# Spare identity matmuls on TensorE inside the four attention cores of a five-block transformer kernel

## What is computed

```python
logits = einsum('bqhd,bkhd->bhqk', q, k) * scale + bias      # causal, band or top-k mask
p = softmax(logits)                                          # B adds a sink to the sum
o = einsum('bhqk,bkhd->bqhd', p, v)
x = x + o @ w_out
x = x + relu(rms_norm(x) @ w_up) ** 2 @ w_down
```

## Time and profile before

| | |
|---|---|
| median of three runs | 1817.03 us |
| the profiled execution | 1824.34 us |
| its span (first to last instruction) | 1822.5 us |
| PE busy | 1723.5 us, 95% |
| DVE, ACT, POOL busy | 1154.3, 930.6, 218.5 us |
| attention cores, about | 36, 37, 34 and 36 us of the span |

### The profile page before, as it was taken

The page is one execution under the profiler, slowest core; times in us unless marked ns, Lnnn a source line. Parts: engine busy times, 40 slices in busy tenths (PEclk is TensorE's granted clock), DMA queues, the critical chain, the costliest instruction groups (busy, mean ns, idle before and its releaser), DMA issues.

```text
span 1822.5 us, 26545 instructions
## 1 busy us (share of the span) xinstructions
PE 1723.5 (95%) x9368; PEld 1459.2 (80%) x9368; DVE 1154.3 (63%) x1958; ACT 930.6 (51%) x1504; POOL 218.5 (12%) x297
## 2 busy tenths in 40 slices
PE   7999999999999988899998899998799999789998
PEld 6889988887788876698886698887598888569887
DVE  6676454556678757755666666567765654875665
ACT  5462354644444554654446554447754445465443
POOL 3005420100000002300003400003100000320000
PEclk9999999999999988999999999999999997899999
DMA  8440046546456442256664156553266664235662
GB/s 273 130 139 1 1 124 179 182 128 196 146 177 196 161 146 81 82 184 186 189 190 151 55 178 193 186 160 120 67 219 188 188 186 127 81 95 184 190 190 81
DMA packets 158450, 270.29 MB, mean 148 GB/s; under 512 B 15181, under 2 KB 42268, under 8 KB 158364
## 3 DMA queue, kind: packets, MB, share of 16 engines
q1 hardware_dynamic: 156843, 263.35, 46.6%
q0 software_dynamic: 1504, 5.79, 0.9%
q10 hardware_dynamic: 16, 0.00, 0.0%
HBM read 268.04 MB, written 1.07 MB: 148 GB/s over the span
## 4 chain that ended last, share of the span: by engine, by line
PE 82%; DVE 8%; ACT 4%; issue 3%; POOL 2%; DMA 0%; DVEq 0%; SPq 0%; ACTq 0%; POOLq 0%
PE p_AC L2479 11%; PE p_AC L2481 11%; PE p_AC L2480 11%; PE p_UP L2479 6%; PE p_UP L2481 6%; PE p_UP L2480 6%; PE p_TP L2512 5%; PE p_UP L2512 5%; PE p_TP L2546 3%; PE p_UP L2513 2%; PE p_TP L2513 2%; PE p_AC L1152 1%; DVE t_wl L1993 1%; ACT t_lg L1520 1%; PE p_UP L1140 1%
## 5 line engine op out<-in xcount | busy, mean ns | idle before, releaser
L1993 DVE TENSOR_TENSOR t_wl<-t_raw,t_wh 128x1024 fp32r<-128x1024 f32 (+2 forms) x525 | 610.5, 1169 | 484.1 <-ACT t_wh L1412 481.4
L1412 ACT ACTIVATE t_wh<-t_raw 128x1024 fp32r<-128x1024 f32 (+2 forms) x525 | 529.6, 1014 | 602.4 <-PE p_AC L2481 290.7
L2479 PE MATMUL p_AC<-t_wh,t_uTh 128*128 128x512 f32 (+1 forms) x612 | 241.5, 395 | 9.5 <-DVE t_uTl L2172 3.9
L2481 PE MATMUL p_AC<-t_wh,t_uTl 128*128 128x512 f32 (+1 forms) x612 | 239.7, 392 | 0.0
L2480 PE MATMUL p_AC<-t_wl,t_uTh 128*128 128x512 f32 (+1 forms) x612 | 239.7, 392 | 0.0
L2479 PE MATMUL p_UP<-t_wh,t_hT 128*128 128x512 f32 (+3 forms) x576 | 227.4, 395 | 4.0 <-DVE t_hT L2038 4.0
L2481 PE MATMUL p_UP<-t_wh,t_hT 128*128 128x512 f32 (+3 forms) x576 | 224.1, 389 | 0.0
L2480 PE MATMUL p_UP<-t_wl,t_hT 128*128 128x512 f32 (+3 forms) x576 | 223.8, 389 | 0.0
L2512 PE MATMUL p_TP<-t_hT,t_wh 128*128 128x512 f32 x384 | 144.4, 399 | 0.0
L2512 PE MATMUL p_UP<-t_hT,t_wh 128*128 128x512 f32 x384 | 144.0, 398 | 0.0
L2479 PEld LDWEIGHTS p_AC<-t_wh,t_uTh 128*128 128x128 f32 x612 | 115.8, 189 | 34.9 <-DVE t_uTl L2172 8.0
(11 more groups left out here) (346 smaller groups left out, 2820.4 us busy)
## 6 DMA issues: line engine op xcount, KB each, us to landing
t_raw<-in_w_up SPq DMA_DIRECT2D x128, 512.0 KB, 3.9
t_raw<-in_w_down SPq DMA_DIRECT2D x128, 512.0 KB, 3.9
t_raw<-in_w_in SPq DMA_DIRECT2D x72, 512.0 KB, 3.6
t_raw<-in_w_up SPq DMA_DIRECT2D x88, 256.0 KB, 3.9
t_raw<-in_a_w_in SPq DMA_DIRECT2D x26, 512.0 KB, 4.3
t_raw<-in_w_down SPq DMA_DIRECT2D x44, 256.0 KB, 3.2
t_raw<-in_a_w_out SPq DMA_DIRECT2D x16, 512.0 KB, 3.4
t_raw<-in_b_w_in SPq DMA_DIRECT2D x12, 512.0 KB, 3.8
```

What stands on the lines that cost most here:

```text
L1412: A_(wh[:, c % SPL, 0:size(c)], raw[:, c % RAW, 0:size(c)], ACT.Copy).then_inc(high_done, 1)
L1993: V.tensor_tensor(wl[:, c % SPL, 0:n], raw[:, c % RAW, 0:n], wh[:, c % SPL, 0:n].bitcast(F32), ALU.subtract).then_inc(split_done, 1)
L2479: M(outs[t], a_hi, w_hi[:, k, :], start=first and k == 0, stop=False)
L2481: ins = M(outs[t], a_lo, w_hi[:, k, :], start=False, stop=last and k == ch.nk - 1)
```

## The change

`spare(count)` issues matmuls of the 128x128 identity with itself, into the last 128 columns of bank 0 of `TP`, which nothing reads and no transpose uses. A matmul is two records, so `spare(2)` is four.

```diff
@@ -2599,6 +2599,11 @@
             def att_core(n):
                 c = att_list[n]
                 hb, pb = AH * n, PAIRS * n
+
+                def spare(count):
+                    for _ in range(count):
+                        M(tpb(0, P, 3 * P), ident[:, :], ident[:, :], start=True, stop=True)
+
                 for i in range(PAIRS + 3):
...
@@ -2613,6 +2618,7 @@
                                          start=True, stop=True)
                         last.then_inc(qk_done, 1)
                     if i == HALF1_STEP[n % 3]:
+                        spare(14)
                         evacuated(pe, layer_blocks[n]["q"][0])
                         query_transposes_pe(pe, transposes, n, 1)
...
@@ -2623,6 +2629,9 @@
                     if n == 2 and i == 3:
                         upto(pe, "q3c_done", 4)
                     if 2 <= i < PAIRS + 2:
+                        if i >= 3:
+                            pe.wait_ge(ev_done, hb + 2 * i - 5)
+                        spare(8 if n == 2 and i < 4 else 2)
                         for h in (2 * i - 4, 2 * i - 3):
                             pe.wait_ge(norm_done, pb + h // 2 + 1)
                             if h >= 2:
```

## The result

With the change the kernel takes 1826.59 us (median of nine executions, 1822.86 to 1829.33 us) against 1819.33 us before (nine, 1817.0 to 1824.27 us). The ratio is 1.0032 with a 95% interval from 1.0016 to 1.0048: 0.32% slower, some 5.8 us. The prediction had 1819.9 us, a loss of 2.9 us on a base of 1817.03 us, with 1814.5 to 1825.5 us as its range. The median of 1826.59 us itself lies above that range, but the base has moved with it, as the same kernel timed more often shows; on the old base the ratio gives 1822.8 us, inside the range. The sign was right, the size half of what was measured, and of the cases the one with 0.36 (slower by over 0.2%) came true by the median, not the one with 0.52; the interval reaches down to 0.16%.

A forecast was written before the change was run, and what follows sets the result against it. Attention cores were taken as bound by POOL, then DVE, ACT and hand-overs (layers 0, 3), and by a PE-DVE-ACT ring (layer 2). Costs 5.54 us less gains 2.63 us, net +2.9 us on 1817.03 us: 1819.9 us, range 1814.5 to 1825.5 us.

The forecast's parts named there:

- the one with 0.52: Whole kernel: time within 0.2% (3.6 us) of before, that is no measurable change; chance 0.52.
- The price of a spare: Any spare group on PE: 0.112 us a record, 0.224 us a matmul; two cost 0.45 us, eight 1.79 us.
- The fourteens: Ahead of DVE's query half in layers 0, 1, 3: 3.14 us, covered; at low clock 1.4 us late as upper end.
- Layer 1: Its core: 0.24 and 1.02 us gained from the clock, two groups on the chain cost 0.9 us; net -0.36 us.
- Layer 0: Its core: +0.45 us for a group behind ACT's copy, about 0.3 us for pushed scores, no clock gain; +0.75 us.
- Layer 2: Its core: second eight +1.79 us, clock gain -1.37 us, three later groups +1.35 us; net +1.77 us.
- The second eight come after ACT's copy: Layer 2, eight spares behind ACT's copy at 1287.80 us, paid in full at full clock: +1.79 us.
- rival C: Clock falls despite spares, as before layer 2's second eight: these take 3.58 us, gains vanish; +7.3 us, 1824.4 us, chance 0.16.
- Layer 3: Its core, same program as layer 0: groups cost 0.75 us together, no gain from the clock.
- So that slow stretch costs nothing that lasts: Layers 0 and 3: 33.44 and 33.40 us despite layer 0's slow step 2, as POOL is late next; clock gain none.
- A: Rival, faster: PE's clock decides in all slow stretches, 13.0 us gained less 5.5 us costs; 1809.5 us, chance 0.10.
- B's figure: Rival, slower: PE's queue becomes the bound, every group of steps 5 to 9 paid; +8.2 us, 1825.2 us, chance 0.14.

The follow-up runs named there:

- the second trace with the change: The change plus 16 extra 512-column products a layer in the narrow projections of layers 0 and 3, against the kernel before: 1818.82 us, ratio 0.9985.

## Why the prediction was half right

**The price of a spare** was right. 28 records took 3.39 us in layer 1, 16 took 1.95 us; with a last record of about 0.28 us that is 0.115 and 0.111 us a record, against 0.112 us predicted. By the figure that I had set beside it, 81 ns a matmul from the Trainium skill, TensorE: Matmul & The Clock Gate, section "Back-to-back issue gap", it would have been 1.3 us for the eight instead of 1.8 us (an estimate, 16 records at 81 ns); the row decided, and rightly.

**The fourteens** are covered, as predicted, in all three layers: what was left of the waits was 1.87, 0.97 and 0.67 us. In layer 3 they took 3.92 us, so the clock rose soon after their start and the 1.4 us for the upper end weren't needed.

**Layer 1** was predicted at -0.36 us and measured at -0.62 us: the query half's transposes took 1.06 us, the clock stayed up at 1020 us, and the copy that step 8 waits for came 1.6 us sooner after the core's start (1.26 us predicted). Both groups at the end are paid, 1.0 us together.

**Layer 0** was predicted at +0.75 us and measured at +0.77 us. The kernels without a group in its steps show that this core varies by 1.6 us by itself (35.82 to 37.39 us), and the second trace with the change had +2.3 us, so the agreement to 0.02 us is luck. Within the trace the terms fit: the copy that step 8 waits for came 0.30 us later after the core's start, its group took 0.54 us, and the last one was covered. That both traces with the change came out longer than their base fits the predicted sign, but two traces don't show it.

**Layer 2** is where the sum failed, by two terms of one step. "The second eight come after ACT's copy at 1287.80 us: +1.79 us" had the place right and the clock wrong: 3.54 us. "In exchange the transposes, values and scores that follow run at full clock", -1.37 us, all but failed: 1.49 us for six transposes, 1.12 us for the values, and from the transposes to the scores 2.74 us against 2.93 us, 0.19 us gained. The groups behind cost about 1.0 us, not the 1.35 us counted, and 3.54 - 0.19 + 1.0 us makes the 4.3 us measured. PE idled 3.11 us ahead of the eight, and spares that stand behind the idle time can't keep up a clock that falls in it. Predicted +1.77 us, measured +4.34 us, and 42.67, 42.69 and 42.82 us in the three traces with the eight in this place. The base is less firm: two of seven traces without a group in this core's steps had some 42 us too. What ties the loss to the eight is that the core fell to 39.53 us without them and to 37.22 us with them ahead of the copy. That is what rival C had said for just this place; I had spread its chance over the whole kernel instead of asking it here, where the idle time was longest.

**Layer 3** failed at an argument. "So that slow stretch costs nothing that lasts" rested on two cores of equal length, one with a slow step 2 and one without. It holds for one slow step: measured from its first scores, core 0 is 0.38 us longer than core 3 in the trace before, and 0.34 us of that is there already when the transposes of step 2 start. With the low clock lasting through the values of step 3, the core took 1.3 us more with no spare in it. The change had such a stretch (values 1.12 us) and put four records more into it, behind ACT's copy, 1.0 us: +2.40 us against +0.75 us, and 38.22 us again in the second trace with the change. Part of this is the trace of before, which had the shortest core 3 of all kernels without groups in the steps (35.98 us, the others 36.33 to 37.31 us).

**The rivals.** A is out in its size: with spares in the right places the cores gained 2.4 to 3.3 us, not 13 us. C, given 0.16, came nearest with +7.3 us to the 6.9 us that the cores lost, and its sign, a clock still at 0.5 behind the spares, was there in layers 2 and 3; in layer 1 it was not. The rule in the Trainium skill, TensorE: Matmul & The Clock Gate, section "HAM oscillation — how this bites in real kernels", that throttled time costs half its length, overstates the cores for the reason given: most of that time isn't on the path. Where PE hardly waits it fits. In the narrow part of layer 3 the low clock lasted about 20 us and cost 9.5 us. B's figure, +8.2 us with twos, wasn't reached: in half of the steps 3 to 9 of the four cores PE still waited ahead of its group. The base was a fault of its own: three executions at 1817.0 to 1819.3 us hid that the same kernel runs from 1813 to 1828 us, so what I called 0.2% was too little for what two medians of this kernel can differ by.

## What to carry to other kernels

Filler work must stand where the engine idles, that is ahead of the wait that ends last, in a buffer that needs no wait of its own. Behind it, it costs its full time and, in layer 2 here, twice that, because the clock had fallen by then. By one trace each, the same 118 matmuls cost the cores 6.9 us behind ACT's copy and gained them 1.3 us ahead of it, though the whole time of that kernel was still 0.20% over before. Before pricing a small edit from two traces, cut both into parts and look at the parts that it doesn't touch; and one pair of equal lengths shows that one slow step is absorbed, not that a longer slow stretch is.

## What the runs showed of the hardware that I had not expected

PE's clock can fall while PE is never idle. In layer 3 of the trace before, PE is busy for 10.00 of 10 us from 1516 to 1526 us and again from 1526 to 1536 us; at 1529.94 us, within a row of 72-column matmuls, their spacing goes from 0.11 to 0.21 us, and the granted clock was then at 0.50 for ten microseconds of full work:

```profile
1530.00:1540.00 10.00, 10.00 (x49) 0.50 0.30 105
```

The same window of the trace with the change had 75 records (0.83). In the eight traces without added work there, core 2 to core 3 took 267.3 to 267.8 us four times, 265.7 us once, 260.3 us twice and 258.0 us once. So this part, which is the same in all eight kernels, has levels some 7 to 9.5 us apart, and what decides between them wasn't found. The busy share of the records doesn't show it. The Trainium skill, TensorE: Matmul & The Clock Gate, Part 1, says that the clock follows how busy PE has been of late; these rows show that a PE that is busy in the records at all times can still be granted half.
